# Norms of the first six layers: h in hi and lo parts written by the layer in front, the factor per token applied to the products

## What is computed

```python
for i in range(DEPTH):                       # 2
    slot = i // N_MIXERS
    x = x + 0.5 * swiglu(rms_norm(x, norm_gains[i, 0]), ffn_w_gate_up[i, 0], ffn_w_down[i, 0])
    h = rms_norm(x, norm_gains[i, 1])
    if i % N_MIXERS == 0:
        x = x + stick_breaking_attention(h, sb_w_in[slot], sb_w_out[slot])
    else:
        x = x + sliding_window_attention(h, positions, sw_w_in[slot], sw_w_out[slot], ...)
    x = x + 0.5 * swiglu(rms_norm(x, norm_gains[i, 2]), ffn_w_gate_up[i, 1], ffn_w_down[i, 1])
```

## Time and profile before

| | us |
|---|---|
| median of three timed runs | 5002.9 |
| lowest and highest | 4979.82 and 5005.48 |
| profiled execution, own time | 4980.36 |
| its span, first to last instruction | 4978.5 |
| PE busy | 4558.2 (92%) |
| VectorE busy | 2417.7 (49%) |
| ScalarE busy | 1423.1 (29%) |
| GpSimd busy | 358.2 (7%) |
| mean granted clock of PE, of full speed | 0.951 |

### The profile page before, as it was taken

The page is one execution under the profiler, slowest core; times in us unless marked ns, Lnnn a source line. Parts: engine busy times, 40 slices in busy tenths (PEclk is TensorE's granted clock), DMA queues, the critical chain, the costliest instruction groups (busy, mean ns, idle before and its releaser), DMA issues. The chain is left out here.

```text
span 4978.5 us, 58886 instructions
## 1 busy us (share of the span) xinstructions
PE 4558.2 (92%) x22233; PEld 3799.0 (76%) x22233; DVE 2417.7 (49%) x3451; ACT 1423.1 (29%) x1506; POOL 358.2 (7%) x213
## 2 busy tenths in 40 slices
PE   8998998998998679988887798889999999999998
PEld 6887657887887568878776687677777888888886
DVE  4323233323323653335666433358887775455554
ACT  2222342222222332223333212233233333222222
POOL 0000000000000000001112000000000000333331
PEclk9998999999998789999998899999999999999998
DMA  3232112322232013222111222245554556555553
GB/s 110 94 91 68 34 34 76 101 90 88 93 92 77 0 51 99 87 81 64 51 45 39 64 76 89 78 142 135 128 138 139 183 166 191 200 190 195 192 192 112
DMA packets 502095, 519.82 MB, mean 104 GB/s; under 512 B 24664, under 2 KB 463060, under 8 KB 500964
## 3 DMA queue, kind: packets, MB, share of 16 engines
q1 hardware_dynamic: 501988, 518.41, 33.9%
HBM read 444.94 MB, written 73.40 MB: 104 GB/s over the span
## 5 line engine op out<-in xcount | busy, mean ns | idle before, releaser
L78 DVE TENSOR_TENSOR w_lo<-w_raw,w_hi 128x2048 fp32r<-128x2048 f32 (+2 forms) x322 | 672.3, 2089 | 1272.2 <-ACT w_hi L72 1272.2
L72 ACT CAST w_hi<-w_raw 128x2048 fp32r<-128x2048 f32 (+2 forms) x322 | 555.5, 1729 | 1136.6 <-PE psum L2836 482.9
L94 PE MATMUL psum<-h_hi_ffn,w_hi 128*128 128x512 f32 x1280 | 497.9, 389 | 0.0
L95 PE MATMUL psum<-h_lo_ffn,w_hi 128*128 128x512 f32 x1280 | 497.9, 389 | 0.0
L96 PE MATMUL psum<-h_hi_ffn,w_lo 128*128 128x512 f32 x1280 | 497.9, 389 | 0.0
L94 PE MATMUL psum<-h_hi_peer,w_hi 128*128 128x512 f32 x1104 | 441.1, 400 | 23.6 <-DVE w_lo L2683 15.9
L96 PE MATMUL psum<-h_hi_peer,w_lo 128*128 128x512 f32 x1104 | 433.8, 393 | 0.0
L95 PE MATMUL psum<-h_lo_peer,w_hi 128*128 128x512 f32 x1104 | 433.8, 393 | 0.0
L2834 PE MATMUL psum<-pr_act_hi,w_hi 128*128 128x512 f32 x1024 | 398.3, 389 | 0.0
L2835 PE MATMUL psum<-pr_act_lo,w_hi 128*128 128x512 f32 x1024 | 398.3, 389 | 0.0
L2836 PE MATMUL psum<-pr_act_hi,w_lo 128*128 128x512 f32 x1024 | 398.3, 389 | 0.0
(11 more groups left out here) (470 smaller groups left out, 8049.8 us busy)
## 6 DMA issues: line engine op xcount, KB each, us to landing
w_raw<-in_ffn_w_gate_up_dram SPq DMA_DIRECT2D x176, 512.0 KB, 4.2
w_raw<-in_peer_u_dram SPq DMA_DIRECT2D x256, 256.0 KB, 5.1
w_raw<-in_peer_v_dram SPq DMA_DIRECT2D x128, 512.0 KB, 4.3
w_raw<-in_w_in_dram SPq DMA_DIRECT2D x64, 512.0 KB, 4.4
peer_hidden<-pr_q SPq DMA_DIRECT2D x64, 512.0 KB, 4.0
peer_gates<-pr_staged SPq DMA_DIRECT2D x8, 4096.0 KB, 12.9
pr_back<-peer_hidden SPq DMA_DIRECT2D x64, 512.0 KB, 6.2
pr_gate<-peer_gates SPq DMA_DIRECT2D x64, 512.0 KB, 7.1
```

What stands on the lines that cost most here:

```text
L72: c.nc.scalar.copy(c.hi[:, slot, :cols], c.raw[:, slot, :cols]).then_inc(c.hi_ready, 1)
L78: c.nc.vector.tensor_tensor(c.lo[:, slot, :cols], c.raw[:, slot, :cols], c.hi[:, slot, :cols].bitcast(F32), ALU.subtract).then_inc(c.lo_re ...
L94: c.nc.tensor.matmul(out, w_hi, x_hi, start=(n == 0), stop=False)
L95: c.nc.tensor.matmul(out, w_hi, x_lo, start=False, stop=False)
```

## The change

The norms of the first six layers are done by a new class `Entry`. The factor per token is no longer in h: h is x times gain alone, in hi and lo. ScalarE writes hi with one Copy that scales by the gain, VectorE lo with one subtraction; a square per chunk on ScalarE and one addition per chunk on VectorE gather the sum of squares in `c.gather`. The layer in front does this for the chunks that it has finished: `ffn` in its down rounds for chunks 0 to 6, `project` for chunks 0 to 5; it also splits the next layer's slot 0 tile. Its last addition to x and the last chunk or two are `left` to the next layer's block, where they come first (`tail_scalar`, `tail_vector`; the root's table is loaded there ahead of them). The very first layer does all eight chunks so. PE does the four summing products behind chunk 5 of the first tile (in the very first layer behind the whole tile) and the widening behind that tile or in the second. `sw` needs no widening.

The factor then goes to the results: in `ffn` VectorE multiplies the gate banks by `c.factor` into `silu`, ScalarE does Silu in place, VectorE the product in place (the tile `a` is gone), and since the up half has no factor of its own, the down result is multiplied by it before it is added to x. In `sb` the values are multiplied by the factor of a token in VectorE's copy, and q and k by `take`, which goes from ScalarE to VectorE. In `sw` all copies multiply. Some semaphores are merged, in numbering only.

In the peer stage ScalarE stages the quads before ahead of its wait for the transpose and its `copy_hi`.

```diff
+class Entry:
+    def scalar(self, act, k):
+        x, gain, hi, _ = self.operands(k)
+        nc, n = self.c.nc, k + self.run * KD
+        nc.scalar.activation(hi, x, ACT.Copy, scale=gain).then_inc(self.hi_done, 1)
+        act.wait_ge(self.gathered, k + (self.run * (KD + 1) + 1))
+        nc.scalar.activation(self.square, x, ACT.Square).then_inc(self.squared, 1)
+    def vector(self, dve, k):
+        x, gain, hi, lo = self.operands(k)
+        nc = self.c.nc
+        dve.wait_ge(self.hi_done, k + (self.run * KD + 1))
+        nc.vector.scalar_tensor_tensor(lo, x, gain, hi.bitcast(F32), ALU.mult, ALU.subtract).then_inc(self.lo_done, 1)
+        dve.wait_ge(self.squared, k + (self.run * KD + 1))
+        dve.wait_ge(self.gathered, k + (self.run * (KD + 1) + 1))
+        nc.vector.tensor_tensor(self.c.gather[:, :], self.c.gather[:, :], self.square, ALU.add
+                                ).then_inc(self.gathered, 1)
+    def tail_scalar(self, act):
+        act.preload_act_table_set("sqrt_and_others")
+        self.wait_tail(act)
+        for k in self.tail:
+            self.scalar(act, k)
+    def sums(self, pe):
+        pe.wait_ge(self.gathered, (self.run + 1) * (KD + 1))
+        for t in range(TC):
+            mm = self.c.nc.tensor.matmul(self.factor[:, t:t + 1], self.c.gather[:, t * P:(t + 1) * P],
+                                         self.c.ones[:, 0:1], start=True, stop=True)
+        mm.then_inc(self.summed, 1)
+    def widen(self, pe):
+        pe.wait_ge(self.steps, self.run * 4 + 3)
+        self.c.nc.tensor.matmul(self.factor, self.c.ones[:, :], self.c.gather[:, :], start=True, stop=True
+                                ).then_inc(self.summed, 1)
...
@@ ffn, ScalarE
-                act.wait_ge(c.tile_used, 2 * (u0 + i) + 3)
-                if not (isinstance(i, int) and i == 0):
-                    act.wait_ge(up_taken, m0 + i)
-                nc.scalar.activation(silu[:, :, :], ps[:, 0:2, :], ACT.Silu).then_inc(gated, 1)
                 split_hi(c, act, u0 + i + 1, 0, cols)
+                act.wait_ge(scaled, i + (s0 + 1))
+                nc.scalar.activation(silu[:, :, :], silu[:, :, :], ACT.Silu).then_inc(gated, 1)
                 act.wait_ge(up_taken, m0 + i + 1)
-                nc.scalar.copy(a_hi[:, bass.ds(i * 2, 2), :], a[:, :, :]).then_inc(a_hi_done, 1)
+                nc.scalar.copy(a_hi[:, bass.ds(i * 2, 2), :], silu[:, :, :]).then_inc(a_hi_done, 1)
...
-            with act.Fori(1, KD) as n:
+            for n in range(1, KD):
                 split_hi(c, act, u1 + n, 0, KH * P)
                 split_hi(c, act, u1 + n, 1, KH * P)
+                if then is not None:
+                    act.wait_ge(out_taken, n0 + n)
+                    then.scalar(act, n - 1)
+            if then is not None:
+                split_hi(c, act, u1 + KD, 0)
@@ ffn, VectorE
+                dve.wait_ge(c.tile_used, 2 * (u0 + i) + 3)
+                if not (isinstance(i, int) and i == 0):
+                    dve.wait_ge(a_hi_done, m0 + i)
+                    dve.wait_ge(a_lo_done, m0 + i)
+                nc.vector.tensor_tensor(silu[:, :, :], ps[:, 0:2, :],
+                                        c.factor[:, :].unsqueeze(1).broadcast_to([P, 2, T]), ALU.mult).then_inc(scaled, 1)
                 split_lo(c, dve, u0 + i + 1, 0, cols)
...
+                nc.vector.tensor_tensor(silu[:, 1, :], ps[:, 4 + bank, :], c.factor[:, :], ALU.mult
+                                        ).then_inc(scaled, 1)
+                dve.wait_ge(scaled, n + (s0 + n_up + 1))
+                nc.vector.scalar_tensor_tensor(x, silu[:, 1, :], 0.5, x, ALU.mult, ALU.add
+                                               ).then_inc(out_taken, 1)
...
@@ ffn, PE
-            pre.tensor(pe)
-            for j in range(2):
-                wait_tile(c, pe, u0, j)
-                products_as_ready(c, pe, pre, wide_jobs(c, h, j))
+            wait_tile(c, pe, u0, 0)
+            w_hi, w_lo = w_tile(c, 0, KD, 256)
+            for k in range(KD):
+                entry.wait(pe, k)
...
+                if k == KD - 3 and len(entry.tail) < KD:
+                    entry.sums(pe)
+            mm.then_inc(c.tile_used, 1)
+            if len(entry.tail) == KD:
+                entry.sums(pe)
+            else:
+                entry.widen(pe)
@@ project
+                then.left((KD - 2, KD - 1), lambda dve: add(dve, pairs - 1, 1),
+                          lambda act: act.wait_ge(added, m0 + 2 * pairs))
@@ sb_attention, VectorE
+                nc.vector.scalar_tensor_tensor(qk[:, m, :], proj, HEAD ** -0.5 if m % 2 == 0 else 1.0, c.factor[:, :],
+                                               ALU.mult, ALU.mult).then_inc(qk_taken, 1)
@@ peer, ScalarE
-                    j = (x + 1) % 2
+                    stage(o, before)
                     act.wait_ge(turned, o * ROUND_UNITS + (SPREAD_AT + x + 2))
-                    copy_hi(j)
-                    stage(o, before)
+                    copy_hi((x + 1) % 2)
                     stage(o, between)
```

More of the change, by code:

```diff
@@ L410, in ffn_first, with ffn @@
     return go
-def ffn(c, tag, gain, w_gu, w_down, h, following):
+def ffn(c, tag, entry, w_gu, w_down, h, following, then):
     nc = c.nc
@@ L637, in project @@
         m0 = run * (2 * pairs)
+        if then is not None:
+            then.square = ph.enter_context(nc.sbuf_tensor(f"square{run}", [P, T], F32))[:, :]
         ps = c.psum
@@ L652, in _ @@
             split_hi(c, act, u0, 1)
-            with act.Fori(1, pairs) as i:
-                for j in range(2):
-                    split_hi(c, act, u0 + i, j)
+            if then is None:
+                with act.Fori(1, pairs) as i:
+                    for j in range(2):
+                        split_hi(c, act, u0 + i, j)
+            else:
+                for part in range(2 * pairs - 1):
+                    split_hi(c, act, u0 + 1 + part // 2, part % 2)
+                    act.wait_ge(added, m0 + part + 1)
+                    for k in range(2 * part, 2 * part + 2):
+                        then.scalar(act, k)
         @block.vector
@@ L800, in body @@
                 for hh in range(4):
-                    if more and hh:
-                        for m in ((0,), (1,), (2, 3))[hh - 1]:
-                            take(i + 1, m)
                     if hh < 3:
@@ L861, in body @@
                 for hh in range(4):
+                    if more and hh:
+                        for m in ((0,), (1,), (2, 3))[hh - 1]:
+                            take(m, i + 1)
                     if more and hh == 0:
@@ L999, with sw_project @@
 SW_QK = SW_HEADS + 2
[L1002 removed]
+def sw_project(c, entry, w_in, h, qk, v, following):
     nc = c.nc
@@ L1021, in _ @@
         def _(act):
-            def splits():
-                for j in range(2):
-                    split_hi(c, act, u0, j)
-            pre.scalar(act, splits)
+            entry.tail_scalar(act)
+            split_hi(c, act, u0, 1)
+            entry.root(act)
             for m in range(1, 3):
@@ L3102, in build @@
         setup(c, w, following[0])
-        for n, layer in enumerate(plan):
+        with ExitStack() as early:
+            c.h = [early.enter_context(nc.sbuf_tensor(f"h_{n}", [P, KD, T], F32R)) for n in ("hi", "lo")]
+            c.gather, c.factor = (early.enter_context(nc.sbuf_tensor(n, [P, T], F32)) for n in ("gather", "factor"))
+            entries = [Entry(c, layer, which) for layer in range(2) for which in range(3)] + [None]
+            for n, layer in enumerate(plan[:6]):
+                layer.run(following[n + 1], entries[n], entries[n + 1])
+                assert c.use == sum(done.uses for done in plan[:n + 1]), layer.name
+        for n, layer in list(enumerate(plan))[6:]:
             layer.run(following[n + 1])
```

319 lines of the change are left out of this document (205 added, 114 removed).

## The result

The changed kernel takes 4862.1 us (4861.6 to 4862.6, 4 runs). Before takes 5003.1 beside it (4979.8 to 5005.5, 4 runs). The ratio is 0.972, with a 95% interval of 0.9706 to 0.9735. Forecast was 4861 with a range of 4820 to 4900, so the number is right. The way to it has one hole: the sum of 141.8 was made on the profiled execution of before, 4980.4, and should have given 4838. The profiled execution of after took 4862.6 (span 4860.8). Between the two profiles lie 118 us, not 142.

What follows compares the result with a forecast made beforehand. TensorE was taken as the bound, busy eight or nine tenths, so only its waits count. Entries 51.0 + 21.7 + 22.7, first norm 8.6, expert stage 39, less 0.75 and 0.5: 5002.9 - 141.8 = 4861 us, range 4820 to 4900.

Steps and rivals of the forecast that it cites:

- the sum of 141.8: Whole kernel: total gain in us, 51.0 + 21.7 + 22.7 + 8.6 + 39 - 0.75 - 0.5.
- Five fed entries: Starts of three feed-forward and two attention layers, prepared by the layer in front: gains 51.0, 21.7 and 22.7 us.
- the gap: I take 0.8: Block edge at a fed entry: PE stands 0.8 us, where 16.7 us passed without a product.
- I take 1.9: Fed entries: the four sums and the widening cost PE 1.9 us at the high clock, bounds 1.9 and 3.9.
- over 3 us: Norms of the five later entries: ScalarE's table load has over 3 us to spare, so a dearer load costs nothing.
- The first norm: Very first layer, nothing in front: PE starts at 21.6 instead of 32.05; gain 8.6 us, bounds 5 and 10.
- I cost both at nothing: 44 feed-forward up units: VectorE's added 1.22 us multiplication before the low part, and the shared buffer, cost 0.
- The expert stage: Staging right after Gelu removes PE's stall of 5.1 us, 3.29 of it idle; gain 8 x 4.9 = 39 us.
- Rival B: Expert stage gains nothing because PE waits for w_lo instead of the staging copy; 39 us back, 4900; chance 0.10.
- Rival A: Layer entries: PE's clock stays low over each, costing some 29 us, 4890; chance 0.10.
- Rival C: Entries: the edge or last chunk holds all chunks, so only the expert stage gains; 4964; chance 0.04.
- it would be 4838; I put the forecast on the median: Whole kernel: profiled 4980.4 would become 4838, but the gain was taken from the timed median 5002.9, giving 4861.

Runs made afterwards that it cites:

- Run 5: The changed kernel without the head start: each of the six layers makes all chunks in its own block, factor still moved to the results; 4911.8 us.
- Runs 6 and 7: The changed kernel with four, then eight, more VectorE passes per up unit ahead of the low part; four: 4867.9 us, eight: 4977.7, 4976.7 and twice 4945.2 us.
- run 1: The kernel before, unedited, timed again: two of 12 executions took 4977.0 and 4977.1 us, ten 5002.7 to 5005.0; the profiled one 5005.0.
- run 3: The changed kernel with ScalarE's old order in the expert stage (weight copy before staging); median 4899.4 us of 4898.4, 4900.4, 4901.7 and 4872.3.
- run 7: The changed kernel with eight more VectorE passes per up unit, ahead of the low part; 4977.7, 4976.7 and twice 4945.2 us.
- run 8: The changed kernel with four filler products before each of PE's 16 waits for normalized weights in the sliding-window attention; 4855.1 us.
- run 12: The changed kernel with 72 filler products before the sliding-window loop, and inside it two before the first head's weight turn and one before each copied-weights wait; 4834.0 us.

## Why the prediction was right, and where it wasn't

*Five fed entries.* Forecast 51.0 + 21.7 + 22.7 = 95.4, measured some 97. Measured singly, by the shift of the same products between the two traces, with the forecast in brackets: sb 22.7 (21.7), sw 23.0 (22.7), the feed-forward ones 17.1 to 17.8 at ffn01 and ffn10 and 16.7 at ffn11, where the mixer's edge is in it (17.0). Of the 22.7 of sb, 21.4 stand at its first scores; the other 1.3 came in the loop over its heads, where the sum had put a loss of 0.5. The step "the gap: I take 0.8" measured 0.77, 0.50, 0.47, 0.50 and 0.47 at the five edges; "I take 1.9" for sums and widening measured 0.95 + 1.02. That the late chunks' work costs nothing was right: the squares were gathered 4.8 us before they were wanted at ffn10, and 3.7 us before at ffn01, behind a projection (by the prediction's own terms 8.2 - 5.5 = 2.7 there, not the "over 3 us" it gives the table load in all five). Run 5 shows what the head start is worth: 49.6 us.

*The first norm.* 8.6 forecast, 7.0 measured. The mis-sized term is PE's start: 21.6 against 23.39. The working had one table load and there are two (1.28 each), and both stand ahead of the first chunk. The first tile made up a little of it: 12.7 us (23.39 to 36.07) where 13.35 were put, with clock 0.84 over its first 11.3 us and no wait but one of 0.3.

*The loops.* "I cost both at nothing" holds: up units take 21.8 us with VectorE busy for 8.2 in place of 6.9. The chain was put at 4.2 to 5.5 and is 4.24. Runs 6 and 7 bound it: four more passes are hidden, eight are not.

*The expert stage.* Forecast 39 (8 x 4.9), measured 39.3 between the two profiles and 36.6 by undoing it alone in after; in the execution of run 1 before needs 1194.5 us between the two marks where it needed 1196.8 in the first profile, so some 37 is the better figure. Rounds are 47.65 where about 47.5 was worked out, and the step that a stall costs more than its idle (3.29) because the clock falls is shown by run 3: 26.3 idle, 36.6 lost. Rival B is refuted, since no wait for w_lo takes the stall's place: from 3683.6 on, just behind the first gate product, PE in after waits for nothing but the last norm.

*Rival A* did not come: the clock is 1.00 in the first 35.9 us of sb and in windows over the four other edges. (So the rule of "TensorE: Matmul & The Clock Gate" in the Trainium skill, Part 1, weighed there, and the trace agree.) *Rival C* neither: PE's gaps at the edges exclude it.

*The level.* The step "it would be 4838; I put the forecast on the median" was the one on which all hung, and it was taken without knowing what the 22.5 us were. They are the two ways of the sliding-window attention (run 1). After takes the long way, seen in its profile and by its time in the other three executions, as most executions of before do. So the sum of differences holds from median to median: 5003.1 - 141 = 4862. The trace of run 1, where before takes the long way too, checks it directly: its span of 5003.1 is 142.3 above after's 4860.8, with the stage the same to 0.4. That both medians have the long way was luck as far as the prediction goes, since nothing in it gave a reason for it. Had after taken the short way, it would have been some 4836 (an estimate, 4862.1 less the stage's 26.3), still in the range. Set against the profiled execution the sum was wrong by 24 us: 26.3 of the stage and 1.6 of the first norm against it, and some 4 for it in the other terms.

*Still open.* What picks the way. Merging semaphores in before gave the short one 10 times of 10, and the same function in after the long one 4 times of 4. The way is not fixed by after's code up to the stage: run 3's kernel is the same up to there, and one of its four executions, like two of run 7's, has a time that fits the short way (no profile shows it). After with the old, unmerged semaphores was not tried.

## What to carry to other kernels

A factor per token that a norm needs can be applied to the results of the products instead, and the rest of the norm done a chunk at a time by the layer in front. The stretch without a layer's product at the edge of sb falls from 16.7 us to 7.3 with the moved factor and chunks alone, and to 0.8 with the head start. Before a forecast is summed on a profiled execution, ask which of the kernel's levels it stands on, and look for the stage that differs. In a stage where PE both waits and is granted a low clock, a few products that nobody reads, put into the waits themselves, can be worth more than they cost; try few, and in each wait.

## What the runs showed of the hardware

- One stage, unchanged, ran at two speeds: 123.9 us at a granted clock of 0.83, or 150.6 at 0.69, with the same instructions. In the long form stretches at 0.50 with PE fully busy alternate with stretches at 1.00 in which PE idles a third of the time (windows of run 8). With some of that idle filled (run 12) the clock of the whole stage was 0.95.
- Filler ahead of the loop (64 products) changed nothing, 4863.9 against 4862.1. Ten products a turn inside it, in two kinds of wait, made the stage 126.8 us; eight a turn in only one kind left it at 145.5. Four a turn in both kinds, with 72 in front of the loop, made it 118.8.
- Small PE operations took half the time at the high clock: the four summing products 1.87 us at clock 0.50 and 0.95 at 1.00, the widening 2.07 and 1.02.
- A stop of PE over a block's edge with nothing late was 0.47 to 0.77 us at the five edges, and the clock stayed at 1.00 over it.
- A copy on ScalarE at the very start had a table load of its own of 1.28 us in front of it (16.64), and the root's set followed with another (19.84). The next activation began 0.02 us behind the load's end (21.14).
